# Decoder step: cache pages loaded as keys and values into separate buffers, from two queues

## What is computed

```python
c_past  = cache_ckv[l][page_table].reshape(DB, -1, KV_RANK)     # latent rows, 256 wide
kr_past = cache_krope[l][page_table].reshape(DB, -1, MLA_ROPE)  # rotary keys, 64 wide
s_past  = einsum('bthr,bsr->bhts', q_lat, c_past) + einsum('bthe,bse->bhts', q_rope, kr_past)
p = softmax(s, -1)
o = einsum('bhts,bsr->bthr', p[..., :P], c_past) + ...
```

## Time and profile before

| | us |
|---|---|
| three runs, median (lowest to highest) | 1549.17 (1538.95 to 1551.23) |
| the profiled execution's own time | 1544.54 |
| its span, first to last instruction | 1542.5 |
| PE busy in it | 1425.7 (92%) |
| ACT busy in it | 415.7 (27%) |
| mean granted TensorE clock | 0.937 |

### The profile page before, as it was taken

The page is one execution under the profiler, slowest core; times in us unless marked ns, Lnnn a source line. Parts: engine busy times, 40 slices in busy tenths (PEclk is TensorE's granted clock), DMA queues, the critical chain, the costliest instruction groups (busy, mean ns, idle before and its releaser), DMA issues.

```text
span 1542.5 us, 21451 instructions
## 1 busy us (share of the span) xinstructions
PE 1425.7 (92%) x8885; PEld 1302.0 (84%) x8885; DVE 622.5 (40%) x936; ACT 415.7 (27%) x665; POOL 96.0 (6%) x65
## 2 busy tenths in 40 slices
PE   7988989969957999879999999999999999999996
PEld 7976778955735766659999999999999999999996
DVE  4122111155457466646565233332423223142548
ACT  3112112350443233335354031220303112030225
POOL 4100000000002000002220000000000000003022
PEclk9999999885977799969999999999999999999998
DMA  7557875422021000112213020120301102020103
GB/s 250 190 173 245 278 258 192 165 97 93 1 74 35 18 9 1 55 41 97 69 28 110 1 81 30 37 72 0 107 2 58 51 27 82 0 85 24 55 0 111
DMA packets 88315, 127.32 MB, mean 83 GB/s; under 512 B 8443, under 2 KB 58773, under 8 KB 88118
## 3 DMA queue, kind: packets, MB, share of 16 engines
q1 hardware_dynamic: 88246, 126.36, 25.0%
HBM read 110.30 MB, written 16.04 MB: 82 GB/s over the span
## 4 chain that ended last, share of the span: by engine, by line
PE 65%; DVE 7%; ACT 4%; issue 1%; POOL 0%; ACTq 0%; DVEq 0%; POOLq 0%
PE psum L1921 22%; PE psum L1949 21%; PE psum L1644 6%; PE psum L1177 5%; PE psum L1888 3%; PE psum L1475 2%; ACT p_rows L1514 1%; DVE pT_lo L1554 1%; PE psum L871 1%; PE psum L1484 1%; DVE softmax_stats L1536 1%; PE psum L875 1%; PE psum L841 1%; PE psum L850 1%; ACT pT_hi L1520 1%
## 5 line engine op out<-in xcount | busy, mean ns | idle before, releaser
L1978 ACT ACTIVATE hid_tmp<-psum 128x1032 f32<-128x1032 f32 x32 | 33.1, 1033 | 531.3 <-PE psum L1921 527.4
L331 PE MATMUL psum<-xTh,win_hi 128*128 128x344 f32 (+1 forms) x432 | 146.1, 338 | 9.4 <-DVE xTl L381 9.4
L1921 PE MATMUL psum<-x_hi,w_hi 128*128 128x344 f32 x720 | 153.3, 321 | 0.0
L1921 PE MATMUL psum<-x_lo,w_hi 128*128 128x344 f32 x720 | 152.8, 320 | 0.0
L1921 PE MATMUL psum<-x_hi,w_lo 128*128 128x344 f32 x720 | 152.0, 319 | 0.0
L1949 PE MATMUL psum<-hid_hi,w_hi 128*128 128x344 f32 x672 | 142.5, 320 | 0.0
L1949 PE MATMUL psum<-hid_lo,w_hi 128*128 128x344 f32 x672 | 142.4, 320 | 0.0
L1949 PE MATMUL psum<-hid_hi,w_lo 128*128 128x344 f32 x672 | 141.8, 319 | 0.0
L331 PE MATMUL psum<-xTl,win_hi 128*128 128x344 f32 (+1 forms) x432 | 140.9, 326 | 0.0
L331 PE MATMUL psum<-xTh,win_lo 128*128 128x344 f32 (+1 forms) x432 | 140.7, 326 | 0.0
L2043 DVE TENSOR_TENSOR z_T<-z_T,psum 128x1032 f32<-128x1032 f32 x48 | 59.0, 1229 | 186.5 <-PE psum L1949 186.5
(11 more groups left out here) (365 smaller groups left out, 2268.0 us busy)
## 6 DMA issues: line engine op xcount, KB each, us to landing
pages<-in_pages SPq DMA_DIRECT2D x128, 288.0 KB, 4.3
mlp_raw<-in_w SPq DMA_DIRECT2D x64, 512.0 KB, 4.3
scratch<-proj_stage SPq DMA_DIRECT2D x17, 516.0 KB, 4.6
win_raw<-in_w_in SPq DMA_DIRECT2D x17, 512.0 KB, 6.4
x_T_raw<-in_x_T SPq DMA_DIRECT2D x6, 688.0 KB, 9.2
z_T<-in_x_T SPq DMA_DIRECT2D x3, 1376.0 KB, 6.1
out_y_T<-z_T SPq DMA_DIRECT2D x12, 344.0 KB, 2.4
wout_raw<-in_w_out SPq DMA_DIRECT2D x8, 512.0 KB, 3.7
```

The source lines that it names most:

```text
L331: mm = pe.matmul(psum[0:M, 3 * (m % 2) + b, 0:BLK], w[:, m % 2, k, 0:M], x[:, k, b * BLK:(b + 1) * BLK], start=(k == 0 and i == 0), stop=( ...
L1921: mm = pe.matmul(psum[:, 3 * (i % 2) + b, 0:BLK], w[:, i % 2, k], x[:, k, C3[b]], start=(k == 0 and n == 0), stop=(k == KD - 1 and n == 2))
L1978: act.activation(ht[:, i % 2, :].rearrange("p (b c) -> p b c", b=3), mlp_set(i), ACT.Relu).then_inc(h_free, 1)
```

## The change

The ring of whole pages becomes two rings in the same memory: `k_pages` (320 columns) and `v_pages` (256 columns). Each page is brought by two DMAs, one for each. SP issues the key halves of unit u+2 after S(u), freed by the score matmuls. ACT issues the value halves of unit u+2 right after it has copied the value bank of unit u, freed by the value matmuls. Both read the page numbers themselves. S(u) waits for its keys and V(u) now waits for its values. Units 0 and 1 are loaded in tiles 1 and 2 as before, values by ACT there too.

```diff
-        pages = sb(GLA_IN, "pages", [P, 2, PG, PW])
+        KW = PW - KVR
+        kpages = sb(GLA_IN, "k_pages", [P, 2, PG, KW])
+        vpages = sb(GLA_IN + 2 * PG * KW, "v_pages", [P, 2, PG, KVR])
...
+        def load_pages(eng, u, dst, lo, done):
+
+            b, hf, _ = unit(u)
+            at_0 = b * PAGES + hf * PG
+            regs = [eng.value_load(pt[0:1, at_0 + j:at_0 + j + 1], min_val=0, max_val=N_PHYS - 1) for j in range(PG)]
+            for j, page in enumerate(regs):
+                src = a["pages"][bass.ds(page, 1)].rearrange("o p c -> (o p) c")[:, lo:lo + dst.shape[-1]]
+                eng.dma_start(dst[:, u % 2, j, :], src).then_inc(done[u % 2], 16)
+
+        def load_k(sp, u):
+            if u >= 2:
+                ds.wait(sp, ("u", u - 2))
+            load_pages(sp, u, kpages, 0, kp_loaded)
+
+        def load_v(act, u):
+            if u >= 2:
+                dq.wait(act, ("val", u - 2))
+            load_pages(act, u, vpages, KW, vp_loaded)
...
-                if p in VALUE_AT and VALUE_AT[p] + 2 < NU:
-                    load_pages(VALUE_AT[p] + 2)
+                if p in SCORE_AT and SCORE_AT[p] + 2 < NU:
+                    load_k(sp, SCORE_AT[p] + 2)
...
                 if m in (1, 2):
                     if m == 1:
                         sp.wait_ge(pt_loaded, 16)
-                    load_pages(m - 1)
+                    load_k(sp, m - 1)
...
+                if m in (1, 2):
+                    if m == 1:
+                        act.wait_ge(pt_loaded, 16)
+                    load_v(act, m - 1)
...
                 pe.wait_ge(pet_done, u + 1)
+                pe.wait_ge(vp_loaded[u % 2], 16 * PG * (u // 2 + 1))
...
-                pe.wait_ge(pg_loaded[u % 2], 16 * PG * (u // 2 + 1))
+                pe.wait_ge(kp_loaded[u % 2], 16 * PG * (u // 2 + 1))
...
                 dq.free(act.activation(o_all[:, unit(u)[2], :], dq.of(key)[:, 0:KVR], ACT.Copy), key)
+                if u + 2 < NU:
+                    load_v(act, u + 2)
```

More of the change, by code:

```diff
@@ L226, in hymba_step @@
             "x_sums", "x_means_stored", "page_table_loaded", "wuq_f32_loaded", "wuv_f32_loaded"))
-        pg_loaded = [sem(f"pages_loaded{i}") for i in range(2)]
+        kp_loaded = [sem(f"k_pages_loaded{i}") for i in range(2)]
+        vp_loaded = [sem(f"v_pages_loaded{i}") for i in range(2)]
         dc_done, dsq_done, dvar_done, drs_done, dn_done, dqn_done, dql_done, qb_zero, qb_done = (sem("decode_" + n) for n in (
@@ L459, in pe_decode @@
                 pe.wait_ge(pet_done, u + 1)
+                pe.wait_ge(vp_loaded[u % 2], 16 * PG * (u // 2 + 1))
                 for j in range(PG):
                     g = j % 4
-                    mm = pe.matmul(dq.of(key)[32 * g:32 * g + 32, 0:KVR], pet[:, u % 2, j, :], pages[:, u % 2, j, PW - KVR:PW],
+                    mm = pe.matmul(dq.of(key)[32 * g:32 * g + 32, 0:KVR], pet[:, u % 2, j, :], vpages[:, u % 2, j, :],
                                    start=(j < 4), stop=(j >= PG - 4))
@@ L477, in pe_decode @@
                         mm = pe.matmul(o[32 * kq:32 * kq + 32, 0:PG * 32].rearrange("p (j c) -> p j c", c=32), qb[:, b, kq, k, :],
-                                       pages[:, u % 2, :, c0:c0 + 32], start=(k == 0), stop=(k == 2))
+                                       kpages[:, u % 2, :, c0:c0 + 32], start=(k == 0), stop=(k == 2))
                 ds.full(mm)
```

## The result

The changed kernel takes 1570.14 us (median of 4 runs, 1564.46 to 1577.32), the kernel before 1548.11 us on the same chips. The ratio is **1.018, 95% interval 1.0134 to 1.0226**: slower, and by more than the 1% that a measurement tells. Forecast were 1566 us and a range of 1538 to 1592. The profiled execution took 1573.21 us (span 1571.2), 28.7 us more than the one of before, so it lies at the upper side of the four.

What follows compares the result with a forecast made beforehand. Pages late through SP's queue time were taken to bound the kernel. V(0) to V(14) was summed as 175.3 + 2 + 4.5 = 181.8 us against 160.3, so 1544.5 + 21.5 = 1566 us, range 1538 to 1592.

Steps and rivals of the forecast that it cites:

- The bound before: At the score matmuls PE waits 19.0 us for late pages, mainly because a unit's load holds SP's queue 9.4 us.
- What the change removes: Keys asked for over 4 us earlier, after S(u), remove the 19.0 us of page waits and slow matmuls behind long ones.
- What it adds: 9.4 us of ACT queue time per unit for eight register reads and eight DMA issues, between 5 and 12 us.
- The chain: From V to V: ACT's copy, value load, exponential, DVE's transpose, 11.8 us; PE waits at every V(u), u 1 to 14.
- The term that was mis-sized: Six V to V intervals with a high split or stage copy, 1.05 us, before the exponential: 6 x 12.85 = 77.1 us.
- The gate term: After period 20 the first gate matmul waits some 3 us for its load; V(4) falls about 2 us behind.
- The lower clock: After pauses over 2.7 us, V takes 2.0 instead of 1.07 us, five times: 4.5 us.
- The sum: V(0) to V(14) takes 181.8 us instead of 160.3, so +21.5 us, carried to the end.
- the two smaller terms: Added to 175.3 us: 2 us for the gate matmul's late load and 4.5 us for PE's lower clock.
- the load costs ACT more: Rival, chance 0.15: two queues issuing together make each ACT load 11 us, +22 more, 1588 us.
- The load costs ACT little: Rival, chance 0.18: an ACT load takes 6 us or less, the kernel gets faster by 10 to 25 us, 1529.
- Even trade: Rival, chance 0.15: ACT's load takes 7 to 8.6 us, page waits become equal transpose waits, 1547 us.

Runs made afterwards that it cites:

- v_pool: Changed kernel with the value halves issued by GpSimd in place of ACT: 1531.9 us, ratio 0.9917 to the kernel before.
- v_pool_keys_late: v_pool, but SP asks for the keys of u+2 only after V(u), as before the change: 1549.1 us, ratio 1.0037 to the kernel before.
- keys_late: Changed kernel, but SP asks for the keys of u+2 only after V(u); values still by ACT: 1571.4 us, ratio 1.0187 to the kernel before.
- lo_behind_max: Changed kernel, but DVE writes the low part of four tiles' weights behind the row maximum instead of ahead of it: 1563.1 us, ratio 1.0102.
- pool_act_16_reads: v_pool plus sixteen register reads for nothing on ACT after each value copy, 8.8 us of its queue: 1574.3 us, ratio 1.0207 to the kernel before.
- act_reads_twice: Changed kernel, but ACT reads the eight page numbers of each unit from 2 on twice, no more DMAs: 1631.8 us, ratio 1.0573.

## Why the prediction was right

Point by point, by its own steps:

- **The bound before.** Late pages because of queue time: right. One reading was loose: from V(u) to S(u+2) it is not "two and a half periods or less" but two periods for half of the units and three for the others. The four long waits, 2.7 to 5.0 us, are all at scores two periods behind (S(2), (5), (9), (13)). v_pool removes the waits with the same bytes, and v_pool_keys_late brings 18.8 of the 19.0 us back by asking later.
- **What the change removes.** The waits at S(u) went whole. That the earlier keys are worth about that much was right, but only a kernel without the chain shows it (11 to 17 us); in the changed kernel they earn nothing in time (keys_late).
- **What it adds.** The load on ACT was priced at 9.4 us from SP's rows and measures 9.0 in the mean. That rows of one queue priced another was the largest risk, and it held: a register read is 275 ns (median) on ACT and 267 on SP, a DMA issue 340 against 333.
- **The chain.** The links are near the forecast where nothing else was put in them: 0-1 takes 10.6, 4-5 11.4, 8-9 10.9, 10-11 12.0, 12-13 11.8 against 11.8, and 5-6 13.1. But PE waited at ten values and not at fourteen. At V(4), (6), (8) and (10) the transpose was there first: PE, slowed after the pause before, was itself behind. And one link was not in the forecast: at V(7), (11), (12) and (14) the copy of the gate's bank stands between transpose and PE, some 0.36 us each.
- **The term that was mis-sized.** "In six a high split or a stage copy of the same size, 1.05 us": in the four with a high split it is 2.93 us from the split's start to the exponential's. I had followed ACT's list and not DVE's: the low part, 1.23 us, waits for the high split and stands on DVE ahead of the maximum that the exponential needs. Those four took 15.9, 15.3, 15.0 and 15.9 where 12.85 stood in the sum, 10.7 us together. DVE's part of that is 4 x 1.88 = 7.5 us. The rest is V(1) and V(13) at the lower clock, the bank's copy in three of the four, and loads a little over 9.4. lo_behind_max, which takes only the low part out of the way, brought 8.4 us. DVE was overlooked in interval 2-3 as well: after the second table load the exponential waited 1.3 us more for DVE's bias, and the interval took 17.3 against 15.6.
- **The gate term** (2 us) did not come. The first gate matmul ran at 140.9 without a wait. But interval 3-4 took 13.6 all the same, since after V(3) PE's matmuls ran at the lower clock and PE itself was behind the chain.
- **The lower clock** was put at five value groups of 2.0 us. It struck eight of them, wholly or partly: V(1), (2), (3), (5), (7), (9), (12), (13). And the length of the pause alone, "over 2.7 us", does not tell which: V(13) took 1.71 after 2.97 us, V(14) 1.07 after 3.29. The trace of before already had such a case beside S(9) (2.73 us, then slow): S(13) at 230.44 waited 3.85 us and took 1.50. What decides it stays open.
- **The sum.** 181.8 us forecast, 187.9 measured. The seven plain intervals took 83.3 us (82.6 forecast), the six with a split or a stage copy 87.4 (77.1), interval 2-3 17.3 (15.6). That is 12.6 us over the 175.3, of which the two smaller terms had 6.5 in them. Loads of 9.0 in place of 9.4 us worked the other way.
- **How near it came in time is partly luck.** The sum was made on the profiled execution of before. Between the two profiled executions the difference is 28.7 us, and 21.5 were forecast; between the medians it is 22.0, because the one trace of before lies under its median and the one of after over it.

Of the rivals, *the load costs ACT more* fell: 9.0 us with SP issuing as well, and pool_act_16_reads is as slow with no DMA from ACT. The rule of the Trainium skill behind it (Perfetto Trace Analysis, DMA Instruction, HWDGE: an issue waits for a lock on the shared generator) would have made the loads longer; single issues of up to 1.1 us are there in ACT's queue, but SP had such ones before, when it alone issued, so no run here shows the lock. *The load costs ACT little* fell with the 9.0 us, but its price (1529) is what v_pool shows when the load is really gone (1531.9), and its DMA bound (282 GB/s) was too low: 299 were carried. *Even trade*, at 7.9 us of queue time, lies between 4.4 (1527, faster than before) and 8.8 (1574, slower); no run narrows it further. On the Trainium skill's sentence that several issuing engines save only sequencer time (DMA: Bandwidth & Descriptors, Issuing engines are not separate DMA queues) the runs agree with the fact and not with its weight: the same number of DMAs with the same bytes goes through two queues in both kernels, and moving the queue time of one of them from ACT to GpSimd is worth 38 us.

## What to carry to other kernels

Price a DMA by the time it holds its issuer's queue, register reads included, and look at what stands behind it in that in-order list; 7 to 9 us of computing in 40 say nothing about whether 9 us at one place are free. Such a cost has a threshold in each interval, its slack: here, with 2.4 us for the rest of the chain, some 8.6 us where V to V is 11.0 on PE and some 3.8 where it is 6.2 (estimates from these distances). Above the slack of nearly all, as in act_reads_twice, 4.3 of each further 4.4 us count, once per link. And when work waits for a moved instruction, follow the list of each engine in the relay, not only that of the engine on which it stands; put issues on the engine whose list nobody waits for.

## What the runs showed of the hardware that was not expected

- Eight register reads and eight DMA issues cost ACT, SP and GpSimd much the same: 9.0, 9.4 and near 9.2 us (GpSimd's reads 284 ns, its issues 536 ns and some 0.6 us apart, so 4.7 us for eight). A single issue is dearer on GpSimd (536 against 333 and 340 ns), a whole unit is not.
- Single register reads take much longer at times, instead of 0.27 us up to 1.9 on SP and 1.6 on ACT in the changed kernel, 1.8 on GpSimd in pool_act_16_reads, and 1.5 on SP in the kernel before. Why stays open.
- The halves, with rows of 1280 and 1024 bytes in place of 2304, were carried as fast as the whole pages or faster: 299 GB/s in a stretch with a DMA share of 0.92, against 282 at 0.84.
